# Two transformer blocks on one core: earlier sums, shared weight splits, grouped spreads and four products of zeros

## What is computed

```python
# first block
n = rms_norm(h, attn_norm_w); proj = n @ w_in
h = h + concat(windowed attention, gated two-way retention) @ w_out
m = rms_norm(h, ffn_norm_w)
h = h + (silu(m @ w_gate) * (m @ w_up)) @ w_down          # D_FF = 2816
# second block
a = rmsnorm(h, g_mix); proj = a @ w_in_2                   # q, k, v, uv, gates
h = h + (gated mix of dilated attention and spatial gating) @ w_out_2
h = h + memory_cross_attention(rmsnorm(h, g_cross), rmsnorm(mem, g_mem), w_q, w_kv, w_o)
h = h + feed-forward(rmsnorm(h, g_ffn)); out = rmsnorm(h, g_final)
```

## Time and profile before

| | us |
|---|---|
| median of 3 runs | 2663.57 (2662.53 to 2663.82) |
| profiled execution, own time | 2663.69 |
| its span | 2661.9 |
| TensorE busy | 2630.7 (99%) |
| VectorE, GpSimd, ScalarE busy | 1777.1, 1584.5, 1110.7 |

### The profile page before, as it was taken

One profiled execution on the slowest core, in us unless ns is written; L12 is line 12 of the kernel. 1 busy time (PEld: TensorE's weight loads), 2 busy tenths in 40 slices (PEclk: granted clock), 3 DMA queues, 4 the chain that ended last, 5 costly groups with the idle time before them and its releaser, 6 DMA issues.

```text
span 2661.9 us, 36644 instructions
## 1 busy us (share of the span) xinstructions
PE 2630.7 (99%) x13442; PEld 2145.0 (81%) x13442; DVE 1777.1 (67%) x2505; ACT 1110.7 (42%) x2152; POOL 1584.5 (60%) x1167
## 2 busy tenths in 40 slices
PE   8999999999999999999999999999999999999998
PEld 6777787878888888878888888888887788888887
DVE  7776775687777777781132447773469877777777
ACT  6644432344444434454443335211445444434443
POOL 3232243478888878667732233557325888878884
PEclk9999999999999999999999999999999999999999
DMA  3111102111121211133211011342101111211112
GB/s 141 33 32 33 45 21 93 55 60 59 57 64 60 64 60 57 55 131 111 85 48 47 25 41 56 134 166 72 64 33 43 58 59 60 72 56 56 60 52 84
DMA packets 110924, 172.98 MB, mean 65 GB/s; under 512 B 7968, under 2 KB 61728, under 8 KB 108576
## 3 DMA queue, kind: packets, MB, share of 16 engines
q1 hardware_dynamic: 100416, 133.20, 15.7%
q10 hardware_dynamic: 10336, 37.49, 3.7%
HBM read 154.93 MB, written 15.73 MB: 64 GB/s over the span
## 4 chain that ended last, share of the span: by engine, by line
PE 93%; DVE 3%; POOL 1%; issue 1%; ACT 1%; DMA 0%; SPq 0%; DVEq 0%; ACTq 0%; POOLq 0%
PE PS L1573 14%; PE PS L1575 14%; PE PS L1574 14%; PE PS L1232 10%; PE PS L1234 9%; PE PS L1233 9%; PE PS L1865 2%; PE PS L1866 2%; PE PS L1867 2%; PE PS L1268 1%; PE PS L1271 1%; PE PS L1269 1%; PE PS L1341 1%; PE PS L1607 1%; PE PS L1367 1%
## 5 line engine op out<-in xcount | busy, mean ns | idle before, releaser
L940 POOL TENSOR_TENSOR WH<-WRAW,CST 128x512 fp32r<-128x512 f32 x150 | 170.9, 1139 | 611.5 <-PE PS L1234 541.3
L1232 PE MATMUL PS<-XH,WH 128*128 128x512 f32 x960 | 395.0, 411 | 0.4 <-DVE XL L3812 0.4
L3509 DVE TENSOR_TENSOR H<-H,PS 128x512 f32<-128x512 f32 x560 | 366.4, 683 | 41.9 <-PE PS L1575 41.8
L1234 PE MATMUL PS<-XH,WL 128*128 128x512 f32 x960 | 376.2, 392 | 0.0
L1233 PE MATMUL PS<-XL,WH 128*128 128x512 f32 x960 | 375.5, 391 | 0.0
L986 POOL TENSOR_TENSOR WL<-WRAW,WH 128x512 fp32r<-128x512 f32 x174 | 260.1, 1496 | 91.1 <-ACT WH L2378 78.0
L986 POOL TENSOR_TENSOR WL<-XX,WH 128x512 fp32r<-128x512 f32 x148 | 197.4, 1335 | 101.9 <-ACT WH L2378 101.5
L1573 PE MATMUL PS<-XH,WH 128*128 128x512 f32 x640 | 249.8, 390 | 1.8 <-ACT ACC L2496 1.4
L1574 PE MATMUL PS<-XL,WH 128*128 128x512 f32 x640 | 249.4, 390 | 0.0
L1575 PE MATMUL PS<-XH,WL 128*128 128x512 f32 x640 | 249.4, 390 | 0.0
L1574 PE MATMUL PS<-PL,WH 128*128 128x512 f32 x624 | 243.2, 390 | 0.0
(11 more groups left out here) (456 smaller groups left out, 6087.7 us busy)
## 6 DMA issues: line engine op xcount, KB each, us to landing
WRAW<-ws SPq DMA_DIRECT2D x84, 512.0 KB, 3.4
WRAW<-ws SPq DMA_DIRECT2D x148, 256.0 KB, 2.6
XX<-ws SPq DMA_DIRECT2D x108, 256.0 KB, 2.7
RAWX<-ws SPq DMA_DIRECT2D x68, 256.0 KB, 2.6
gate_spill<-TG ACTq DMA_DIRECT2D x28, 256.0 KB, 2.1
H<-xT ACTq DMA_DIRECT2D x2, 2048.0 KB, 9.6
h_spill<-H ACTq DMA_DIRECT2D x1, 4096.0 KB, 12.9
THB<-gate_spill ACTq DMA_DIRECT2D x4, 1024.0 KB, 5.3
```

The lines of the kernel that those rows point to most:

```text
L940: pool.tensor_tensor(WH[:, j, c], WRAW[:, j, c], ONES[:, 0:1].to_broadcast((P, 512)), ALU.mult).then_inc(hi_split, 1)
L1232: pe.matmul(out, WH[:, j, w], rh(kt), start=(n == 0), stop=False)
L1234: last = pe.matmul(out, WL[:, j, w], rh(kt), start=False, stop=(n == len(kts) - 1))
L3509: dve.tensor_tensor(x, x, PS[:, 4 + t], ALU.add).then_inc(h_added, 1)
```

## The change

Five edits, made together.
- SQ's first half is cleared on VectorE ahead of the 1.0 in STAT, and TensorE multiplies it by itself four times into the bank MB before its first real product; nothing reads the result. one_made counts one more everywhere.
- At the start ScalarE makes the second unit's weight highs after the first two XH instead of before them.
- second_half issues the four spreads in a row at (1, 0) instead of one at each of four tiles.
- In the fast stages the first sum of block 2 moves from P1 of block 2 to the lows of the inputs (behind tile 7), and waits for the column sum that frees ACC instead of for the lows; so that its two quarters are there, the pieces of block 2 are in the order A22, A21, A11, A12 (piece_order). In the mix the first sum of block 3 moves from behind P3 to behind P4.
- In the cross attention three of the four weight highs of the first two query units go to ScalarE (QUERY_HIGHS). norm_sums moves from tile 2 to tile 4, the sum of squares behind step 4, norm_inverse from step 5 to step 6, and ScalarE's norm_root behind step 4.

```diff
@@ -76,6 +76,7 @@
 FFN_AT = (U_FFN1, W_FFN2)
 EARLY = [MEM_AT[5], CQ_AT[2], MEM_AT[6], MEM_AT[7], CQ_AT[3]]
+QUERY_HIGHS = [(u, q) for u in CQ_AT[:2] for q in range(2)]
 MIX_UNITS = [W_GATE + 3 * i for i in range(1, KT)] + [W_G, W_G + 2, W_G + 4]
@@ -104,6 +105,13 @@
 QUARTERS = ("A11", "A21", "A22", "A12")
+
+
+def piece_order(b):
+
+    return ("A22", "A21", "A11", "A12") if b == 2 else QUARTERS
+
+
 GROUPS = ("P1", "P2", "P6", "P5", "P7", "P3", "P4")
 D_GROUPS = ("P1", "P6", "P7", "P4", "P2", "P5", "P3")
 FAST = FT - 2
@@ -179,7 +187,7 @@
 MIX_DONE, MIX_SLOT, MIX_PLACE, MIX_AFTER, N_MIX_DONE = group_tables(MIX_SEQ)
 N_MIX_SLOT = len(MIX_SLOT)
 MIX_SLOT_OF = {n: key for key, n in MIX_SLOT.items()}
-MIX_PIECE_OF = [("plain" if b < 2 else "fast", b, q) for b in range(MIX_BLOCKS) for q in QUARTERS]
+MIX_PIECE_OF = [("plain" if b < 2 else "fast", b, q) for b in range(MIX_BLOCKS) for q in piece_order(b)]
 MIX_PIECE = {key: r for r, key in enumerate(MIX_PIECE_OF)}
 N_MIX_PIECE = len(MIX_PIECE)
@@ -191,7 +199,7 @@
-PIECE_OF = [("plain" if b < 2 else "fast", b, q) for b in range(FT) for q in QUARTERS]
+PIECE_OF = [("plain" if b < 2 else "fast", b, q) for b in range(FT) for q in piece_order(b)]
 PIECE = {key: r for r, key in enumerate(PIECE_OF)}
 N_PIECE = len(PIECE)
 D_LOADS = ("A11", "A21", "A22", "again", "A12")
@@ -929,7 +937,7 @@
                     pool.tensor_tensor(WH[:, 0, c], WRAW[:, 0, c], STAT[:, 95:96].to_broadcast((P, 512)), ALU.mult).then_inc(hi_split, 4)
                     pool.wait_ge(hi_split, 4)
                 else:
-                    pool.wait_ge(one_made, 1 + 2 * j + q)
+                    pool.wait_ge(one_made, 2 + 2 * j + q)
                 pool.tensor_tensor(WL[:, j, c], WRAW[:, j, c], WH[:, j, c].bitcast(F32), ALU.subtract).then_inc(unit_split, 1)
             def split_unit(i, j):
@@ -950,7 +958,7 @@
                 pool.wait_ge(hi_split, 2 * u + 2)
                 pool.tensor_tensor(WL[:, j, c], WRAW[:, j, c], WH[:, j, c].bitcast(F32), ALU.subtract).then_inc(unit_split, 2)
-            pool.wait_ge(one_made, 1)
+            pool.wait_ge(one_made, 2)
             for j in range(2):
                 for q in range(2):
                     first_split(j, q)
@@ -1008,9 +1016,14 @@
                         pool.wait_ge(x_high, (XS_F1, XS_F2)[f] + n + 1)
                         xh, xl = plain_input(n % 8, n // 8)
                         pool.tensor_tensor(xl, scaled_input(n % 8, n // 8), xh.bitcast(F32), ALU.subtract).then_inc(x_low2, 1)
+                        if n == 7:
+                            first_sum(f, 2)
             def first_sum(f, b):
-                pool.wait_ge(w_low, W_LOW_AT[f] + (SLOT["fast", b - 1, "P5"] + 1 if b > 2 else 8))
+                if b > 2:
+                    pool.wait_ge(w_low, W_LOW_AT[f] + SLOT["fast", b - 1, "P5"] + 1)
+                else:
+                    pool.wait_ge(col_sum, 4 + 6 * f)
                 raw_loaded(pool, f, "fast", b, "A21")
                 raw_loaded(pool, f, "fast", b, "A22")
                 pool.tensor_tensor(S1, raw_of("fast", b, "A21"), raw_of("fast", b, "A22"), ALU.add).then_inc(w_sum, 1)
@@ -1034,7 +1047,6 @@
                 if b == 2 and name == "P1":
                     pool.wait_ge(gate_mul, 44 * f + 1)
-                    first_sum(f, b)
                     third_sum(f, b)
                 if b == 2 and name == "P7":
@@ -1151,7 +1163,6 @@
                 a11, a12 = mix_raw("fast", b, "A11"), mix_raw("fast", b, "A12")
                 s = MIX_SLOT["fast", b, name]
                 if b == 2 and name == "P1":
-                    mix_first_sum(b)
                     mix_third_sum(b)
                 mix_low(s)
                 if name == "P1":
@@ -1162,7 +1173,7 @@
                     pool.wait_ge(w_low, N_SLOT + s + 1)
                     pool.wait_ge(w_sum, 4 * at + SUM_AT["S2"])
                     pool.tensor_tensor(a12, a12, a11, ALU.subtract).then_inc(w_sum, 1)
-                if name == "P3" and b + 1 < MIX_BLOCKS:
+                if name == "P3" and 2 < b < MIX_BLOCKS - 1 or name == "P4" and b == 2:
                     mix_first_sum(b + 1)
                 if name == "P4" and b + 1 < MIX_BLOCKS:
                     mix_third_sum(b + 1)
@@ -1180,6 +1191,8 @@
                         pool.wait_ge(x_high, XS_GMIX + n + 1)
                         xh, xl = plain_input(n % 8, n // 8)
                         pool.tensor_tensor(xl, scaled_input(n % 8, n // 8), xh.bitcast(F32), ALU.subtract).then_inc(x_low2, 1)
+                        if n == 7:
+                            mix_first_sum(2)
             i = U_FFN1 // 2
             for j in range(2):
                 pool.wait_ge(raw_in[j], 16 * i + 16)
@@ -1189,10 +1202,20 @@
                     pool.tensor_tensor(WH[:, j, c], WRAW[:, j, c], ONES[:, 0:1].to_broadcast((P, 512)), ALU.mult).then_inc(hi_split, 1)
                     pool.wait_ge(hi_split, 4 * i + 2 * j + q + 1)
                     pool.tensor_tensor(WL[:, j, c], WRAW[:, j, c], WH[:, j, c].bitcast(F32), ALU.subtract).then_inc(unit_split, 1)
-            with pool.Fori(i + 1, EARLY[0] // 2) as i:
+            with pool.Fori(i + 1, CQ_AT[0] // 2) as i:
                 for j in range(2):
                     split_unit(i, j)
-            split_unit(EARLY[0] // 2, 0)
+            split_unit(CQ_AT[0] // 2, 0)
+            for u, q in QUERY_HIGHS:
+                i, j, c = u // 2, u % 2, slice(512 * q, 512 * q + 512)
+                if (u, q) == QUERY_HIGHS[0]:
+                    pool.wait_ge(raw_in[j], 16 * i + 16)
+                    pool.wait_ge(full[2 * j + 1], i)
+                    pool.tensor_tensor(WH[:, j, c], WRAW[:, j, c], ONES[:, 0:1].to_broadcast((P, 512)), ALU.mult).then_inc(hi_split, 4)
+                    pool.wait_ge(hi_split, 4 * i + 2 * j + 4)
+                else:
+                    pool.wait_ge(early_high, QUERY_HIGHS.index((u, q)))
+                pool.tensor_tensor(WL[:, j, c], WRAW[:, j, c], WH[:, j, c].bitcast(F32), ALU.subtract).then_inc(unit_split, 1)
             for u in EARLY:
                 second_part(u)
             for j in range(2):
@@ -1323,6 +1346,10 @@
                     unit_half(u, h, first_half_norm(k, 4, 5) if h else None)
+            pe.wait_ge(one_made, 2)
+            for n in range(4):
+                pe.matmul(PS[:, MB], SQ[:, 0, 0:P], SQ[:, 0], start=True, stop=True)
+
             def scores1(s):
                 b, j = step1(s)
                 k0, nk = window(b)
@@ -1540,8 +1567,9 @@
                 if h == 0 and kt == 4:
                     r_sums(1)
-                if h == 1 and kt < 4:
-                    r_spreads(4 + kt)
+                if (h, kt) == (1, 0):
+                    for n in range(4, 8):
+                        r_spreads(n)
             def residual(u0, xs, k, between):
                 first_units(u0, xs, between=between)
@@ -1967,7 +1995,7 @@
                 last.then_inc(vm_turned, 1)
             def cross_norm(h, kt):
-                if (h, kt) == (0, 2):
+                if (h, kt) == (0, 4):
                     norm_sums(3, 1)
                 if (h, kt) == (0, 6):
                     norm_spread(3, 1)
@@ -2126,20 +2154,24 @@
             act.dma_start(H[:, 0:2, half(0)], xT[:, 0:2, half(0)]).then_inc(x_in, 16)
             act.dma_start(H[:, 2:4, half(0)], xT[:, 2:4, half(0)]).then_inc(h_part[0], 16)
             act.dma_start(x_piece(H, 1), x_piece(xT, 1)).then_inc(h_part[1], 16)
-            act.wait_ge(one_made, 1)
+            act.wait_ge(one_made, 2)
             act.activation(STAT[:, 57:58], STAT[:, 95:96], ACT.Copy)
             for q in (2, 3):
                 act.dma_start(x_piece(H, q), x_piece(xT, q)).then_inc(h_part[q], 16)
-            for j, q in ((0, 1), (1, 0), (1, 1)):
+            def first_weights(j, q):
                 act.wait_ge(raw_in[j], 16)
                 c = slice(512 * q, 512 * q + 512)
                 act.activation(WH[:, j, c], WRAW[:, j, c], ACT.Copy).then_inc(one_made, 1)
+            first_weights(0, 1)
+
             def x_highs(q):
                 act.wait_ge(h_part[q] if q else x_in, 16)
                 for i in range(4):
                     if (q, i) == (0, 2):
+                        first_weights(1, 0)
+                        first_weights(1, 1)
                         act.wait_ge(h_part[0], 16)
                     kt, h = 4 * (q % 2) + i, half(q // 2)
                     high(XH[:, kt, h], H[:, kt, h], v(V_N1 + kt))
@@ -2900,15 +2932,19 @@
                     act.activation(MH[:].rearrange("p a b -> p (a b)"), XX[:], ACT.Copy).then_inc(mem_high, 1)
-            norm_high(3, 2, 4)
+            def first_part_high(u, q=0):
+                i, j, c = u // 2, u % 2, half(q)
+                act.wait_ge(raw_in[j], 16 * i + 16)
+                act.wait_ge(full[2 * j + 1], i)
+                act.activation(WH[:, j, c], WRAW[:, j, c], ACT.Copy).then_inc(early_high, 1)
+
+            norm_high(3, 2, 3)
+            for u, q in QUERY_HIGHS[1:]:
```

(20 more changed lines are left out.)

## The result

The changed kernel takes 2669.99 us in the median of 20 runs (2665.88 to 2673.87), the kernel before 2664.28 us (2662.37 to 2668.52). The ratio is 1.002, 95% interval 1.0013 to 1.0026. That is 5.7 us more, just beyond the 5.3 us that I had called apart from no change, and above the range of the prediction (2659.8 to 2667.2). The profiled execution took 2670.62 us, its span is 2668.7 us.

The account below looks back on a forecast made before the run. TensorE, busy 2630.7 of 2661.9 us, was taken as the bound, so only waits could be won. Terms -1.65 - 0.3 + 3.2 - 0.4 - 0.8 = 0.05, from 2663.69 less 0.1 to the median, gave 2663.6 us; range 2659.8 to 2667.2.

Parts of the forecast that it names:

- two quarters that are there: Feed-forwards' early first sum of block 2: its two input quarters have already landed, so moving it was costed at nothing.
- Part 3: First sum early in both feed-forwards: a later quarter for block 3 delays the down product, +1.6 us each, +3.2.
- part 4: The same early-sum move in the mix: less waiting for the TR tile, -0.4 us (-0.6 to +0.8).
- Rival (c): Start: zeros don't raise the clock (2664.3 us, chance 0.11), or it falls again during waits (2666.6 us, chance 0.07).
- the row of 17 products in 4 us: Before's trace at 1858 to 1862 us: the clock stayed up with few products, taken as evidence against a falling clock.
- slower by over 0.2%: Whole kernel above 2668.9 us, needing a contention-slowed GpSimd chain with a fallen clock or a later landing; chance 0.05.
- (b): Feed-forwards: GpSimd's nine instructions keep their 12.57 us under contention, +3.1 us twice, 2666.6 us; chance 0.12.
- A22 of block 3 is late: Feed-forwards: this quarter, issued only after P4's low, takes 4.2 us to land, at 559.1 us, holding GpSimd.
- The start: Zeros and first tiles in front: product 13 at 13.3 us, norm sums near 21.5 us, -1.65 us (-2.7 to 0).
- The spreads: Four spreads in a row save steps in and out, limited by VectorE's chain: -0.3 us (-1.1 to 0).
- The query weights: Cross attention: three highs on ScalarE bring GpSimd's lows earlier, XL then being late: -0.8 us (-1.5 to -0.2).
- The rows by which I said the forecast would fall: Signs of a wrong forecast: norm sums at 23.13 us don't move, or the wait before the down products disappears.

Follow-up runs that it names:

- mix_at14: The changed kernel with the feed-forwards as before and the mix's early first sum behind tile 14 instead of tile 7: 2663.49 us, 0.9999 of before.
- fill12: The changed kernel plus twelve unread products before the first down product of each feed-forward, inside TensorE's wait: 2668.09 us, 1.0013 of before.
- ffn_back: The changed kernel with both feed-forwards' part undone (old quarter order, first sum of block 2 back in P1), mix's part kept: 2665.62 us, 1.0005 of before.
- a21_ffn: The changed kernel with the mix as before and the feed-forwards' block 2 quarters in the order A21, A22, A11, A12: 2665.04 us, 1.0006 of before.
- cross_back: The changed kernel with the feed-forwards', mix's and cross attention's parts undone, leaving start and spreads in a row: 2664.03 us, 1.0003 of before.
- mix_back: The changed kernel with only the mix's part undone (old quarter order, first sums back in their old places): 2665.69 us, 1.0007 of before.
- nozeros: The changed kernel with only start, spreads and query weights kept, less TensorE's four products of zeros: 2662.16 us, 0.9994 of before.

## Why the prediction was wrong

**Where it failed first: "two quarters that are there".** Part 3 costed the early sum at nothing, since GpSimd waited for ScalarE anyhow, and part 4 took "the same move" over. In the feed-forward it was so: the sum started at 503.12 us without a pause. In the mix the quarter had been issued at 1146.97 us and took 10.3 us, which the trace of before shows in its DMA issues; tile 7's low ended 4 us before that landing. I read the landing of the quarter that I knew to be late, and not of the one that I moved the reader in front of. The price is a wait of 3.4 us, and the mix's term was +4.2 us for -0.4 us. In it are the 6.8 us at the lower level. Without the late quarter (mix_at14) it is +0.6 us, within my bounds, on the wrong side.

**The clock after a wait.** The sum counted waits only. Rival (c) had looked at a falling clock for the start alone, and had let the row of 17 products in 4 us speak against it; a place where TensorE waits 3 us and does two or three products was never compared with that. The step that failed here is the cost of nothing for the clock behind a wait. By the places of the table that cost was 1.3 and 0.8 us in the feed-forwards (fill12) and 1.6 us for one of the two lower stretches in the mix (ffn_back); taken twice there, some 5.3 us in all. That is an estimate, and by it the changed kernel would lie near 2664.7 us with the clock up, inside the range: this term, more than the mix's wait, took the time out of it. The forecast missed the measured time by 6.4 us; 0.7 us of that is the median of before, 2664.28 us in 20 runs against the 2663.57 us of the three that I started from. The time lies in the case "slower by over 0.2%", to which I gave 0.05, but not for its reasons: the clock fell behind the new waits, and (b) had no part. The Trainium skill (TensorE: Matmul & The Clock Gate, "What's actually happening") says that the lower level is what idling restores; I cited it for the start, and the place for it was the wait that I had just put into both feed-forwards. This trace agrees, with 0.50 behind each of the three waits, though the second wait of a21_ffn had none behind it; and fill12 shows for the feed-forwards that TensorE's standing still is the cause and not something beside it: eight of nine such waits in the profiles had the lower level behind them, and neither of the two that were filled.

**The feed-forwards, +1.6 each for +2.3 and +2.4.** The step "A22 of block 3 is late" was right: SP issued it behind P4's low, it landed 3.7 us later (I took 4.2), and the chain from L1029 to L1088's end took 12.5 us (12.35 in my working). What failed is who stands behind it. I put TensorE's wait at the second down product (the low of 570.69 us); it is at the first, whose low stood at 560.51 us and now stands at 561.06 us. Before, that low was ready 0.7 us ahead of TensorE (GpSimd, then TensorE, in the trace of before):
```profile
560.51 1.75 POOL L986 TENSOR_TENSOR WL<-XX,WH 128x512 fp32r<-128x512 f32 x1
562.92 0.39 PE L1573 MATMUL PS<-PH,WH 128*128 128x512 f32 x1
```
The prediction did not look at how little room this first low had.
By then TensorE has gained 1.8 us at start and spreads, 0.4 us for TR and 1.0 us at P4, so it stands there from 559.6 us. In terms of the first feed-forward: +3.3 for the wait, +1.7 for the clock, -0.4, -1.0, and -0.9 for two short waits behind it that are gone, +2.7 for a measured +2.3; the clock's term is the one that comes out smaller. Where the clock stayed up, in a21_ffn's second feed-forward, the sum of all this was +1.1 us, inside the bounds of part 3; that +1.6 would have been near it is luck, since the forecast had the wait at another product and counted the gains ahead of it as nothing. Rival (b), a chain slowed by contention, had no part: the chain took no longer than in my working.

**Right.** The start: -1.53 for -1.65, norm sums at 21.60 us for 21.5. But I gave it to two causes that turned out to be one gain. The spreads: -0.2 for -0.3, by the place in the trace; no run undid them alone. The query weights: -1.0 (1.2 by cross_back) for -0.8; the wait that stays there is still for GpSimd's lows, now of line 1218, 0.53 and 0.20 us, and not for XL as I had said, since these lows took 1.73 us each (four in 6.93 us). P4 of block 2 started without a wait, as said, but only because the sum that used to disturb VectorE was late.

The rows by which I said the forecast would fall did not show it: the norm sums moved, and the wait before the down products did not go but came sooner.

## What to carry to other kernels

Before moving the reader of a load forward on an engine that works in order, look up where that very load lands in the trace, at each place that the same code runs; a move that is free in one stage held GpSimd for 4.6 us in another. In a ring, a piece loaded earlier takes the place of another that must then come later: order the pieces for the whole ring, and put the urgent one ahead of the burst. And where TensorE bounds the kernel, expect a stretch at the lower clock behind a wait of some 3 us: here 3.4 or 6.8 us of it, at 0.8 to 1.6 us for each 3.4. If the wait can't be removed, products that nobody reads, put into it, keep the clock.

## What was not expected of the hardware

- Of nine waits of TensorE of 2.7 to 3.4 us in these profiles, four had 3.4 us at the lower level behind them, four 6.8 us, and one (a21_ffn, second feed-forward) none. The place does not decide it: behind the wait in the first feed-forward stood 3.4 us in the changed kernel and 6.8 us in mix_back, behind that in the mix 6.8 us in the changed kernel and 3.4 us in ffn_back. The wait of 1.6 us for TR in the mix had none behind it in the eight profiles that have it. Near the end, waits of 0.96 to 1.21 us with a norm's small products around them were followed by the lower level in five profiles, and waits of 0.6 to 1.2 us at the same place in seven others were not. What decides between them stays open here.
- The kernel before loses to this too, though not in its profile: of its 33 runs beside mix_back eight took 2666.5 to 2669.7 us, all at a mean granted clock of 0.996, and the other 25, of 2661.7 to 2665.3 us, had 0.997 or 0.998.
- The zeros raised the clock at 5.1 to 7.4 us by the profiles of the versions that have them, against 13.1 us in nozeros and 14.9 us before; the start of nozeros was the same to 0.1 us.
- A load of 256 KB took 10.5 us from issue to landing beside a spill of 4096 KB, against 3.7 us for the one issued at 552.76 us. It landed 0.3 us after the spill, in the trace of before too. That the spill is the cause was not tried.
